# Mixture-of-experts stage: token rows gathered from DRAM, another order of the experts, and sixteen weight buffers at the start

## What is computed

```python
logits = (xt @ w_router).astype(jnp.float32)      # 256 tokens, 8 experts
top_v, top_e = lax.top_k(logits, TOP_K)           # 2 experts for each token
gates = jax.nn.softmax(top_v, axis=-1)
...                                               # rows sorted by expert, padded to blocks of 128
def run(args):
    xb, e = args
    return _swiglu(xb, w1[e], w3[e], w2[e])       # (silu(x w1) * (x w3)) w2, widths 1024, 3584, 1024
...
y = jnp.zeros((T, D), x.dtype).at[stok].add(yb[dest] * sg[:, None].astype(x.dtype))
```

## Time and profile before

| what | value |
|---|---|
| runs | 2617.88, 2619.31, 2616.28 us, median 2617.88 |
| the profiled execution's own time | 2616.33 us |
| its span in the profile | 2614.5 us |
| PE busy | 2507.5 us, 96% of the span |
| DVE, ACT, POOL busy | 1267.4, 941.4, 167.3 us |
| HBM read | 622.38 MB |
| granted PE clock | 1.00 in all stretches shown |

### The profile page before, as it was taken

One profiled execution on the slowest core, in us unless ns is written; L12 is line 12 of the kernel. 1 busy time (PEld: TensorE's weight loads), 2 busy tenths in 40 slices (PEclk: granted clock), 3 DMA queues, 4 the chain that ended last, 5 costly groups with the idle time before them and its releaser, 6 DMA issues.

```text
span 2614.5 us, 64738 instructions
## 1 busy us (share of the span) xinstructions
PE 2507.5 (96%) x29598; PEld 2003.3 (77%) x29598; DVE 1267.4 (48%) x1714; ACT 941.4 (36%) x1227; POOL 167.3 (6%) x169
## 2 busy tenths in 40 slices
PE   8999999999999999899999989999899999999999
PEld 7977799798787666476666556787779978877997
DVE  6678655566871010010100101478577857756785
ACT  4455443355540000000000000356446646654663
POOL 1000000000000000000000000203400000260000
PEclk9999999999999999999999999999999999999999
DMA  6344855555449999999999999733035455313542
GB/s 221 144 162 158 315 178 183 156 181 175 154 161 392 412 413 387 420 420 419 420 417 398 419 419 411 261 135 114 20 138 194 157 175 182 106 52 122 178 170 105
DMA packets 93125, 630.15 MB, mean 241 GB/s; under 512 B 11136, under 2 KB 12400, under 8 KB 23088
## 3 DMA queue, kind: packets, MB, share of 16 engines
q1 hardware_dynamic: 85392, 598.61, 59.0%
q0 software_dynamic: 5760, 24.86, 3.4%
q10 hardware_dynamic: 1696, 2.49, 0.3%
HBM read 622.38 MB, written 11.93 MB: 243 GB/s over the span
## 4 chain that ended last, share of the span: by engine, by line
PE 75%; DVE 11%; DMA 6%; ACT 4%; issue 2%; POOL 0%; SPq 0%; DVEq 0%; ACTq 0%
PE ps L1074 26%; PE ps L795 13%; PE ps L797 13%; PE ps L796 13%; DMA raw<-in_units_dram 5%; DVE wlo L1991 3%; ACT whi L1516 1%; PE ps L1366 1%; PE ps L1146 1%; DMA unit<-in_units_dram 1%; ACT s L1871 1%; PE ps L1345 1%; PE ps L1377 1%; DVE s L2347 0%; DVE mx L2309 0%
## 5 line engine op out<-in xcount | busy, mean ns | idle before, releaser
L1991 DVE TENSOR_TENSOR wlo<-raw,whi 128x2048 fp32r<-128x2048 f32 (+5 forms) x250 | 532.3, 2138 | 306.8 <-ACT whi L1516 306.4
L1516 ACT ACTIVATE whi<-raw 128x2048 fp32r<-128x2048 f32 (+4 forms) x252 | 447.8, 1780 | 203.2 <-PE ps L797 187.9
L797 PE MATMUL ps<-xTh,wlo 128*128 128x256 f32 x1480 | 418.4, 283 | 0.0
L795 PE MATMUL ps<-xTh,whi 128*128 128x256 f32 x1480 | 417.8, 282 | 0.0
L796 PE MATMUL ps<-xTl,whi 128*128 128x256 f32 x1480 | 416.5, 281 | 0.0
L2531 DVE TENSOR_TENSOR hb<-ps,hb 128x384 f32<-128x384 f32 (+1 forms) x56 | 29.4, 525 | 735.9 <-ACT hb L1692 735.9
L1074 PE MATMUL ps<-unit,xe 128*32 128x256 f32 x5248 | 290.9, 379 | 9.3 <-DMA unit<-in_units_dram 9.3
L795 PEld LDWEIGHTS ps<-xTh,whi 128*128 128x128 f32 x1480 | 279.1, 189 | 0.8 <-issue 0.7
L796 PEld LDWEIGHTS ps<-xTl,whi 128*128 128x128 f32 x1480 | 279.6, 189 | 0.1
L797 PEld LDWEIGHTS ps<-xTh,wlo 128*128 128x128 f32 x1480 | 277.3, 187 | 0.0
L1074 PEld LDWEIGHTS ps<-unit,xe 128*32 128x32 f32 x5248 | 179.4, 110 | 116.8 <-DMA unit<-in_units_dram 12.6
(11 more groups left out here) (595 smaller groups left out, 3504.7 us busy)
## 6 DMA issues: line engine op xcount, KB each, us to landing
raw<-in_units_dram SPq DMA_DIRECT2D x358, 1024.0 KB, 6.5
unit<-in_units_dram SPq DMA_DIRECT2D x186, 1024.0 KB, 16.9
raw<-in_units_dram SPq DMA_DIRECT2D x18, 512.0 KB, 3.6
raw<-in_units_dram SPq DMA_DIRECT2D x6, 768.0 KB, 7.1
raw<-in_units_dram SPq DMA_DIRECT2D x8, 544.0 KB, 3.6
raw<-in_units_dram SPq DMA_DIRECT2D x6, 688.0 KB, 4.0
g<-in_b_gate_dram POOLq DMA_DIRECT2D x16, 256.0 KB, 7.9
raw<-in_units_dram SPq DMA_DIRECT2D x4, 576.0 KB, 4.4
```

The costliest lines, as they stand in the source:

```text
L795: self.e.matmul(out, ah, bh, start=start, stop=False)
L797: return self.e.matmul(out, al, bh, start=False, stop=stop)
L1516: self.e.activation(self.m.hi[self.pair(u)][:, 0:n], self.m.raw[self.p.land[u]][:, 0:n], ACT.Copy) \
L1991: self.e.tensor_tensor(self.m.lo[self.pair(u)][:, 0:n], self.m.raw[self.p.land[u]][:, 0:n], self.m.hi[self.pair(u)][:, 0:n].bitcast(F32), ...
```

## The change

1. The layer's input `x` (256 rows) is written to a DRAM tensor `rows_x` by two DMAs of POOL at step `rows`. A new step `index` multiplies `sel` by the token numbers `tok` on PE (four products with two columns), DVE copies the result to `idx`, and POOL gathers the expert's rows from `rows_x` by indirect DMA into `xg`. `lift` now turns these rows with 8 transposes in place of 16 products. For the first expert 256 rows are gathered, for the others 96 or 64.
2. RANKS and FEW: the experts with at most 64 tokens stand second and seventh, where they stood third and seventh.
3. The experts' units use four more buffers once (`early`, the first four units) and one more in a ring of 12 (`more`, for 24 rounds; it shares its place with `yg`). The last 44 units use the ring of 11.
4. `tok`, `sel` in another float type, `hb` and `hTe` in exchanged places, and the waits that go with it.

```diff
+EARLY = 4
+MORE = [RING + EARLY + k_ for k_ in range(1)]
-FEW = {2: 64, 6: 64}
-RANKS = (0, 1, 6, 2, 3, 4, 7, 5)
+FEW = {1: 64, 6: 64}
+RANKS = (0, 6, 1, 2, 3, 4, 7, 5)
@@ Plan: where a unit lands
+        own, six = [(first + k) % NRAW for k in range(NRAW)], list(range(NRAW, RING))
+        lands = [RING + k for k in range(EARLY)]
+        for k in range(28):
+            lands += (MORE if k < 24 else []) + own + six
+        self.lent = first + max(k for k, b in enumerate(lands) if b in MORE)
@@ Plan: order
-            o += [("places",), ("route",), ("counts",)] + pr[2][0:1] + [("begin",)] + pr[2][1:2] + [("lift", 0)]
+            o += [("index", 0), ("places",), ("route",), ("counts",)] + pr[2][0:1] + [("begin",)] + pr[2][1:2] + [("lift", 0)]
...
+                if cb == 2 and ex < 7:
+                    o += [("index", ex + 1)]
@@ Tensor
+    def index(self, ex):
...
+        e.wait_ge(*self.at("sel", ex))
+        if ex == 0:
+            e.wait_ge(*self.at("tok"))
+        for h in range(2):
+            for q in range(2):
+                ins = e.matmul(ps[:, 2 * h:2 * h + 2], m.sel[:, q, 128 * h:128 * h + 128], m.tok[:, q, :], start=(q == 0), stop=(q == 1))
...
     def lift(self, ex):
-        self.e.wait_ge(*self.at("sel", ex))
+        e.wait_ge(*self.at("xg", ex, 0))
...
-                ins = self.chosen(ps, k, 0, self.slots(ex) if self.tiles == 1 else 128)
+                ins = e.transpose(ps[:, k * 128:k * 128 + n], m.xg[0:n, 0, k * 128:k * 128 + 128], m.ident[0:n, 0:n])
@@ Vector
+        elif what == "index":
...
+            e.wait_ge(*self.at("full", "idx", ex))
+            e.tensor_copy(m.idx[:, :], self.psum("idx", ex)[:, 0:4:2]).then_inc(*self.up("d_moe", ("idx", ex)))
@@ Pool
         elif what == "rows":
-            e.wait_ge(*self.at("ln", "m1", 1))
+            for t in range(2):
+                e.wait_ge(*self.at("ln", "m1", t))
+                self.load(("xd", t), w["xd"][128 * t:128 * t + 128, :], m.x[:, t, :])
...
+        elif what == "index":
+            ex = a[0]
+            e.wait_ge(*self.at("idx", ex))
+            if ex == 0:
+                for t in range(2):
+                    e.wait_ge(*self.at("ld", "xd", t))
+            else:
+                e.wait_ge(*self.at("full", "e13", ex - 1, 0))
+            if ex and self.tiles == 1:
+                n = self.slots(ex)
+                self.taken("xg0", ("xg", ex, 0), m.xg[0:n, 0, :], w["xd"], m.idx[0:n, 0:1])
+                return
+            for h in range(2):
+                self.taken(f"xg{h}", ("xg", ex, h), m.xg[:, h, :], w["xd"], m.idx[:, h:h + 1])
@@ Sync
             b, v = p.land[u], p.prior[u]
+            if b >= RING and v < 0:
+                e.wait_ge(*self.at("ln", "m1", 1))
```

More of the change, by code:

```diff
@@ L212, in moe @@
                 self.idf, self.more = t("idf", [1, 8], F32, c1), t("more", [1, 2, 8], F32, c1)
-            self.hTe, self.hb = t("hTe", [128, 28, 256], F32, c0), t("hb", [128, 2, 2, 512], F32, c0)
-            self.yb = t("yb", [128, 2, 1024], F32, c0)
-            self.xe, self.selg = t("xe", [128, 8, 256], F32, c0), t("selg", [128, 2, 352], F32, c0)
+                self.units += [t(f"early{k}", [128, 2048], F32, c1) for k in range(EARLY)] + more
+            self.hb, self.hTe = t("hb", [128, 2, 2, 512], F32, c0), t("hTe", [128, 28, 256], F32, c0)
+            self.yb, self.selg = t("yb", [128, 2, 1024], F32, c0), t("selg", [128, 2, 352], F32, c0)
             self.selg3 = t("selg3", [128, 3, 256], F32, c0)
+            t("apart6", [128, 1088], F32, c0)
+            self.xe = t("xe", [128, 8, 256], F32, c0)
     def second(self, t, hl, c):
@@ L317, in __init__ @@
         self.land, self.prior = [], []
[L318 removed]
+        user, raws, first = {}, 0, self.whole.index(True)
+        own, six = [(first + k) % NRAW for k in range(NRAW)], list(range(NRAW, RING))
[3 more added lines that the diff above has]
+        self.lent = first + max(k for k, b in enumerate(lands) if b in MORE)
         for u, whole in enumerate(self.whole):
[L320 removed]
             halves = [NRAW + u % NHL, NRAW + NHL + u % NHL]
[L322 to L323 removed]
+            if whole:
+                self.land.append(lands[u - first])
             else:
                 self.land.append(raws % NRAW)
[L326 removed]
+            raws += self.land[u] < NRAW
             self.before.append(max(user.get(b, -1) for b in halves))
@@ L755, in do @@
             self.counts()
+        elif what == "index":
+            self.index(*a)
         elif what == "lift":
@@ L1141, in count_tokens @@
         ins.then_inc(*self.up("mm_route", ("full", "pos")))
-    def chosen(self, ps, k, h, n):
-        for q in range(2):
-            ins = self.e.matmul(ps[:, k * 128:k * 128 + n], self.m.x[:, q, k * 128:k * 128 + 128], self.m.sel[:, q, h:h + n],
-                                start=(q == 0), stop=(q == 1))
-        return ins
+    def index(self, ex):
+        e, m, key = self.e, self.m, ("idx", ex)
+        ps = self.fill(key, key)
+        e.wait_ge(*self.at("sel", ex))
[4 more added lines that the diff above has]
+                ins = e.matmul(ps[:, 2 * h:2 * h + 2], m.sel[:, q, 128 * h:128 * h + 128], m.tok[:, q, :], start=(q == 0), stop=(q == 1))
+        ins.then_inc(*self.up("mm_route", ("full",) + key))
     def lift(self, ex):
+        e, m = self.e, self.m
         ps = self.fill(("xe", ex), ("xe", ex, 0), ("xe", ex, 1))
-        self.e.wait_ge(*self.at("sel", ex))
+        e.wait_ge(*self.at("xg", ex, 0))
+        n = self.slots(ex) if self.tiles == 1 else 128
         for c in range(2):
             for k in range(4 * c, 4 * c + 4):
-                ins = self.chosen(ps, k, 0, self.slots(ex) if self.tiles == 1 else 128)
+                ins = e.transpose(ps[:, k * 128:k * 128 + n], m.xg[0:n, 0, k * 128:k * 128 + 128], m.ident[0:n, 0:n])
             ins.then_inc(*self.up("turned_moe", ("full", "xe", ex, c)))
     def upper(self, ex):
+        e, m = self.e, self.m
         ps = self.fill(("xu", ex))
@@ L2091, in do @@
             self.select(a[0])
+        elif what == "index":
+            ex = a[0]
+            if ex:
+                for h in range(2 if ex == 1 else self.tiles):
+                    e.wait_ge(*self.at("xg", ex - 1, h))
+            e.wait_ge(*self.at("full", "idx", ex))
+            e.tensor_copy(m.idx[:, :], self.psum("idx", ex)[:, 0:4:2]).then_inc(*self.up("d_moe", ("idx", ex)))
         elif what == "places":
@@ L2694, in select @@
         else:
-            e.wait_ge(*self.at("full", "xe", ex - 1, 1))
-            if self.tiles == 2:
-                e.wait_ge(*self.at("full", "xu", ex - 1))
+            e.wait_ge(*self.at("full", "idx", ex - 1))
         if ex == 7:
@@ L3061, in do @@
                 e.wait_ge(*self.at("stored" if self.tiles == 1 else "stored_all", 6))
+                e.wait_ge(*self.at("unit", self.p.lent))
             for s in range(2):
@@ L3065, in do @@
             e.wait_ge(*self.at("full", "e13", 7, 0))
+            for h in range(self.tiles):
+                e.wait_ge(*self.at("xg", 7, h))
             self.rows(("fg", 1), m.fg1[:, :], w["ln_ffn_g"][1:2, :], 1024)
```

28 lines of the change are left out of this document (17 added, 11 removed).

## The result

The changed kernel takes 2622.72 us in the median of 12 runs (2620.06 to 2626.66), beside 2617.13 us for the kernel before in 12 runs: a ratio of 1.0021, with an interval of 1.0014 to 1.0029. It is slower by 5.6 us, where 8.7 less were forecast, and lies above the range. The profiled execution has 2622.82 us, 6.5 above the one of before, with a span of 2621.0 us.

What follows compares the result with a forecast made beforehand. The prediction took the DMA to bound the kernel up to unit 293, at the seventh expert's end; 7.0 - 5.9 + 7.6 = 8.7 us less gave 2609.2 us, range 2602.5 to 2618.5.

Steps and rivals of the forecast that it cites:

- the third rival: Expert stage: PE is the bound, not the DMA, so all PE savings show, 17 us, giving 2601 us; chance 0.07.
- Head start: Before the experts, 765 to 790: extra buffers let 4.5 MB more load early, 2.95 MB of it weights; 7.0 us gained.
- Gathers (5.9 us lost): Expert stage: seven later gathers move 2.49 MB, priced by bytes at the full DMA rate; latency hidden; 5.9 us lost.
- the fifth rival: Expert stage: every gather holds the full DMA longer than its bytes; 2 us more each give 2625 us; chance 0.06.
- Ring full (7.6 us gained): Large experts: DMA stops for lack of a free buffer, a 9.6 us shortfall, shrink to 2.0 us; 7.6 us gained.
- theory B of the run with products: That run's own forecast: full-ring pauses let lagging DMA engines catch up, so buffers and order save nothing; 2614 to 2617 us.
- First gather: Before the first expert's lift: gather lands 9.2 us after issue, first product at 791.5; 0 taken, upper end costs 7.4 us.
- the 793 that were free: First expert: first product may start up to 793 without cost; beyond that each us of delay costs one.
- rivals 2 and 4: First gather lands late, 7.4 us given back, 2616.6, chance 0.25; or also held until DVE's chain ends, 2621.7, chance 0.07.

Runs made afterwards that it cites:

- the version without later gathers: Changed kernel without the seven later gathers; experts from the second on lift the rows the first gather left: 2609.65 us, ratio 0.9973.
- The 128-row run: Changed kernel with 128 rows gathered for every expert from the second on, in place of 96 or 64: 2616.24 us, ratio 0.9998.
- 48 partitions with 8 KB each: Changed kernel with the later gathers replaced by plain POOL loads of the same bytes in 8 KB pieces, into half as many partitions: 2625.41 us, ratio 1.0031.
- the version with products: Kernel before with the change's buffers and expert order, keeping the old 16 products of a lift, without index and gathers: 2609.59 us, ratio 0.9971.
- order alone: Kernel before with only the small experts moved to second and seventh place; 11 buffers and products as before: 2614.15 us, ratio 0.9992.
- ring of 13: Kernel before with the new buffers and expert order, old products, and a second `more` buffer in the place of `xg` for 23 rounds: 2605.94 us, ratio 0.9957.
- buffers alone: Kernel before with only the four early buffers and the ring of 12; products and expert order as before: 2615.08 us, ratio 0.9994.

## Why the prediction was wrong, point by point

**What held.** That the DMA sets the time up to the end of the seventh expert: PE waits at the second expert (943.60 to 993.08; forecast 950 to 988) and in the seventh, its waits for units rose from 27.3 to 37.4 us, and the difference of 6.2 us was made before 1542. PE's savings of some 17 us didn't show as a gain, which excludes the third rival. **Head start**: forecast 4.5 MB more from 760 to 790, measured 4.6; less 1.55 MB for the store and the first gather that is 7.3 us, where 7.0 were forecast. A short lift costs 0.85 or 0.71 us, and `index` 0.6, as taken; the gap behind a short lift is 0.3 to 0.7 us instead of 0.1.

Two steps failed, and they are of about the same size. The change was forecast at -8.7 us and came out at +5.6. Against the version without later gathers these cost 7.2 us more than their term, and that version gains 6.9 us where the two other terms promised 14.6.

**The first step that failed: "Gathers (5.9 us lost)", priced by bytes.** Measured against the version without them they cost 13.1 us. The step is "I price them by bytes, since in the stretch with four indirect fetches (0.5 MB each) the DMA moved 418 GB/s". The row was read rightly, but those fetches fill all 128 partitions of `yg`, and the gathers fill 96 or 64 of `xg`. The 128-row run shows what this is worth: 415 GB/s in the changed kernel become 418 or 419 over 900 to 1300, and the time falls by 6.5 us with more bytes. One landing costs (419 - 327) x 4.8 + (419 - 415) x 4.8 = 0.46 MB of rate, 1.1 us, over its own 0.39 MB, 0.9 us. PE's timeline has 1.94 us for one. The mechanism is that of the fifth rival, which had a chance of 0.06; its price of 2 us more than the bytes for each was twice the measured 1.0. By the rival's own working some 1 us more each only uses up the gain, so that this step alone would leave the kernel near its old time and not 5.6 us slower.

By the Trainium skill, SBUF — State Buffer (Door 1: The DMA port swizzle), partitions 0 to 63 reach 8 of the 16 ports, and 96 partitions put 64 rows on one half of the ports and 32 on the other. The runs agree in direction: 128 rows have no dip, and 48 partitions with 8 KB each have the deepest. They don't agree in size: by that rule alone the fuller half takes 64 x 4 KB at 209.5 GB/s, 1.25 us for each gather of 96 or 64 rows and 8.8 for seven (an estimate from that page's port count and the measured 419 GB/s), against 13.1. Stores of as many rows from 96 partitions (`rows_y<-yb`, two pairs in the same stretch of 1108 to 1300) leave no slice under 411 outside the gathers' landings, and that a write and a read of SBUF differ here wasn't tried. So that the number of partitions decides is shown; that the ports are the reason is not.

**The second step that failed: "Ring full (7.6 us gained)".** It takes the whole shortfall of the mean rate, 9.6 us, as time that the stage loses, and all of it but 2.0 us as a gain. The mean rate did go up nearly as forecast. Over 790 to 1538 the shortfall against 419 GB/s is now (15 x 30 + 22 x 80 + 4 x 100 + 5 x 108 + 4 x 192 + 4 x 146 + 4 x 92) / 419 = 11.6 us. The seven landings are 7.7 of it; 3.9 remain, most of it in 790 to 900, where PE runs the first expert at its own pace with a full ring. The prediction let the ring fill there only at the end of its lead; the head start had filled it already. For the fourth to sixth place it was right: 1300 to 1446 has 415, one landing and no stop. (Without gathers the DMA is further ahead and the stops are longer: the version with products has 386, 382, 417 and 402 GB/s over 790 to 820, 820 to 900, 900 to 1000 and 1300 to 1446, a shortfall of 15.8 us. Hence 6.6 us from buffers and order there, and not 14.6.)

But a unit can be used only when the last of its 16 parts has landed, and the mean rate says nothing of that. A DMA's semaphore is counted up 16 times, once for each part, and the traces keep the time of each count. From 1000 on the parts of a unit fall into an early eight and a late eight in all traces, and the late ones drop behind while the stream runs without a stop: by 5.2 to 8.0 us from 1000 to 1300 in each of the versions below, with and without gathers. The gap in the table is the mean time of the late eight less that of the early eight, read from the unit that landed nearest to the time; the last two columns are for the last unit of the seventh expert:

| version | GB/s, 1300 to 1446 | gap at 1300 | gap at 1446 | gap, last unit | its last part behind the mean of the 16 |
|---|---|---|---|---|---|
| order alone | 399 | 8.3 | 0.8 | 2.1 | 1.9 us |
| products, buffers and order | 402 | 10.4 | 1.8 | 3.5 | 2.1 us |
| ring of 13 | 406 | 10.2 | 4.1 | 5.5 | 3.4 us |
| before | 408 | 7.4 | 3.3 | 5.0 | 3.5 us |
| no later gathers | 411 | 10.5 | 8.3 | 9.9 | 6.1 us |
| buffers alone | 412 | 7.5 | 6.4 | 7.8 | 4.5 us |
| changed | 415 | 10.7 | 13.8 | 15.4 | 9.2 us |
| 128 rows | 417 | 10.4 | 14.2 | 14.9 | 7.8 us |

Where a full ring stops the stream, the gap closes, most at the lowest rates; where nothing stops it, it opens further. So in these stops the late eight catch up, and part of the shortfall was never lost time, as theory B of the run with products had it. That the stops cause this is read from eight traces side by side; no run changes the stops alone. In the changed kernel the stops are gone from 900 on, and the last part of that unit comes 9.2 us behind the mean of its 16 parts, where it came 3.5 behind it before. These 5.7 us are in no term of the prediction, and they take back the 5.7 us by which the full ring did shrink (9.6 - 3.9). Which engines are the late ones, and why they are slower, the traces don't tell.

**First gather.** It was issued at 780.95 and 782.39, the wait for it ended at 791.08, 10.1 us after the first issue instead of 9.2, and products began at 792.79: 1.3 us later than forecast, within the 793 that were free. So rivals 2 and 4 didn't happen; no landing in the changed kernel took above 12.3 us, against their 18.1. Whether the first gather is free is open. The medians of the versions without later gathers and with products, which have it and don't, differ by 0.06 us. Their two traces come to the experts at the same time (last routing product at 790.98 and 791.02), and there the version with the gather is 2.3 us behind at the last unit of the second expert (995.37 against 993.03) and 3.1 at that of the seventh (1535.30 against 1532.25), and only the spans of the whole kernel are level again (2612.7 and 2612.8 us).

**The sum once more**, with measured terms, for the last unit of the seventh expert: -7.3 for the head start, +5.9 for bytes, +7.7 for the landings, and -(9.6 - 3.9) = -5.7 for the full ring is +0.6, and with +5.7 for the last part it is +6.3. Measured is +6.2. The two halves can be read apart: the mean landing of that unit's 16 parts moved from 1532.30 to 1532.74, by +0.4, and the rest is the last part. For the ring of 13, with products, the rates give -10.1 (4.2 MB more from 760 to 790, and no store or gather) - 9.6 + 10.6 (its windows of 387 and 406) = -9.1, the mean landing moved by -9.1, the last part by -0.1, and measured is 1526.62 - 1535.84 = -9.2. For 128 rows it closes less well: the rates give -7.3 + 8.8 - (9.6 - 5.3) = -2.8 (5.3 from its windows: 401, 403, 418, 419, 419, 417, 420), the mean landing moved by -4.0, the last part by +4.3, and measured is 1536.15 - 1535.84 = +0.3. A rate rounded to 1 GB/s can hide 0.9 us over 750 us, and the 9.6 leave out 1300 to 1400, where the kernel before has 414 GB/s, 1.2 us more; so these sums are no better than 1 or 2 us. One thing stays open: with 128 rows PE's timeline shows units 1.9 us late at a gather (3.51 + 3.36 - 2 x 2.49), though no slice of the rate dips and the bytes are worth 1.25.

A caution on the traces: those of the versions without later gathers, with products and with buffers alone reach the experts 2.5 to 4.3 us later than all others (last routing product at 790.9 to 791.0, elsewhere 786.8 to 788.4), which nothing in their edits explains, and each was the slowest execution of its version; the trace with 128 rows was the fastest of its own. Differences of absolute times between traces are therefore worth less than the medians.

## What to carry to other kernels

In a stage where a stream of weights fills the DMA, price each added transfer by what it takes from the stream, and look for a row with the same number of partitions, not only the same kind of instruction; here 96 or 64 partitions cost about twice their bytes, and 128 hardly more than once. A shortfall of the mean rate is not all lost time: look at when the last part of a piece lands, since pauses let late parts catch up. Where the DMA sets the time, as here, moving work from PE to the DMA lost even though PE was busy for 95% of the span. More prefetch buffers seem to pay where a consumer that is faster than the stream comes soon enough to empty them: order and buffers gained 2.1 and 1.2 us alone (each within the noise) and 6.6 together, and a ring of 13 with the old products gained 10.6.

## What was unexpected of the hardware

A DMA share of 1.03 together with 338 GB/s: the share says that the engines are occupied, not that they move bytes at the full rate.

The 16 parts of a unit land up to 17.6 us apart (the last unit of the seventh expert in the changed kernel), in two groups of eight, while the mean rate is 415 GB/s or more and each window looks full.

The granted clock fell after PE's wait for the first gather. Three windows of the changed kernel:

```profile
788.00:792.70 4.70, 0.85 (x8) 0.70 (x8) 0.73 (x2) 1.23 (x2) 0.00 (x0) 0.96 1.00 405
792.70:798.00 5.30, 5.21 (x72) 3.00 (x76) 1.49 (x2) 0.00 (x0) 0.00 (x0) 0.71 1.01 424
798.00:804.00 6.00, 6.00 (x120) 3.69 (x116) 0.00 (x0) 0.00 (x0) 0.00 (x0) 1.00 1.01 422
```

Ahead of it PE had been idle for 3.12 us, then busy for 0.85, and idle again for 0.85. The mean of 0.71 is a mix of the two levels, 1.2 and 2.4 GHz, and from 798 on the clock is the higher one again. The first four units took 804.62 - 792.79 = 11.83 us instead of 4 x 2.59 = 10.36, so the wait cost 1.5 us more of PE's time than its length. The same shows at the gather in the seventh expert: behind the wait of 2.21 us at 1477.14, above, 32 products take 2.42 and 2.81 us in place of 1.93, and the granted clock from 1475 to 1490 is 0.89. The second costs nothing, since PE waits for units again right behind it. The first falls where PE sets the pace with a full ring, and may be a part of what the first gather costs.
